# Output projection that starts on attention's half while the recurrence's rows are gated, and first routing weights split inside it

## The chip, the cores and the metric

The kernel runs on one core of one Trainium2 chip. The metric is the device time in microseconds; lower is better. The core has a matrix engine (TensorE; PE in the rows, with its weight loads as PEld), VectorE (DVE), ScalarE (ACT), GpSimd (POOL), and SyncE (SP), which here issues nearly all transfers. The engines run their own instruction streams and meet at semaphores.

## What is computed

One layer of a hybrid decoder on 512 tokens of width 2048, with 16 learned tokens in front: a projection into attention's and a recurrence's inputs, sliding window attention (8 heads of 128), a gated linear recurrence (8 heads of 128) whose outputs are normalised per head and multiplied with a gate, an output projection of both side by side (2048 x 2048), and then a feed-forward part that scores 16384 experts by product keys, picks 16 for each of 8 routing heads and mixes them. All in float32.

```
    _, o = lax.scan(_hgrn2_chunk_step, s0, xs)
    o = o.transpose(1, 0, 3, 2, 4).reshape(B, Lp, HGRN_HEADS, HGRN_DV)[:, pad:]
    o = rms_norm(o, norm_g.reshape(HGRN_HEADS, HGRN_DV)).reshape(B, L, HV)
    return (o * jax.nn.silu(hg.astype(jnp.float32))).astype(out_dtype)
...
        hn = rms_norm(h, ln_mix_g[l])
        proj = hn @ w_in[l]
        aq, ak, av, hq, hf, hi, hg = jnp.split(proj, split_at, axis=-1)
...
        att = sliding_window_sink_attention(aq, ak, av, attn_sinks[l])
        rec = hgrn2_mixer(hq, hf, hi, hg, lbs[l], hgrn_norm_g[l])
        h = h + jnp.concatenate([att, rec], axis=-1) @ w_out[l]
...
        h = h + peer_ffn(rms_norm(h, ln_ffn_g[l]), peer_w_q[l], peer_sub_keys[l], peer_u[l], peer_v[l])
```

## The kernel before

The kernel is a row of stages, each a block of its own: every engine runs its part of a block, and the next block begins when all are done. In order: norm_rows (first norm), project, attend, recur, mix_out (the output projection), norm_rows again (the norm in front of the feed-forward part), route, gate_table, experts. The first five are over at 1023 us of the profiled execution and the second norm at 1048.

**Numbers in two parts.** A float32 matrix product is done as three matmuls on numbers split into a high part (a cast to fp32r) and a low part (the rest): high by high, low by high, high by low (product, L341 to L345). So whatever TensorE multiplies is first split. Class Stream does it for weights: SyncE loads steps of 512 KB (2 chunks of 128 rows by 512 columns) into four raw slots, ScalarE casts the high part (L298; L304 for the first two steps of a stage), GpSimd subtracts for the low part (L312), each into one of two slots, and TensorE counts a step as used when its last matmul is done (used), which opens the slot to ScalarE again. A load into a raw slot waits until the low part that was read from it is done.

**recur.** Eight heads, one after the other, with all engines in turn. When a head's output is in PSUM (o_bank), ScalarE squares and sums it into stat (L1049) and copies it to mix (L1052), whose 2048 columns are attention's 1024 (chunks 0 to 7) and the recurrence's 1024 (chunks 8 to 15). After the last head: SyncE starts the first four loads of w_out, VectorE turns the sums into means, ScalarE takes the root (L1084, with a table load), VectorE makes the reciprocal root (inverse_root, L102 to L106) and then gates: 32 scalar_tensor_tensor instructions of 128 x 128, one for each head and block of 128 tokens (L1231).

**mix_out.** TensorE transposes mix, chunk by chunk: 4 transposes of 128 x 128 each (L1274) into one of 4 PSUM banks; ScalarE casts a bank to mixT_high (L1298), VectorE subtracts to mixT_low (L1323), and the bank is free for chunk c + 4. When all 16 are done (`pe.wait_ge(low, DC)`), the product runs: 4 pieces of 512 output columns, each 8 steps of 2 chunks, each step 2 x 4 x 3 = 24 matmuls of 512 columns. For each piece VectorE adds x (L1333), which SyncE loads into h when all chunks are transposed (L1258; h lies where mix was), and ScalarE squares the sum for the next norm's means (L1304). SyncE's queue is in order: x, then w_out's other steps, then the first four loads of w_q, routing's weights.

**Second norm.** VectorE scales the rows (L206, four instructions of 128 x 2048), TensorE transposes them (L230), ScalarE and VectorE write the two parts (L171, L212). ScalarE and GpSimd split the first two steps of w_q here, ahead of their other work of this block (L168, L181); GpSimd then makes plain_rows (L2139).

**route.** TensorE computes the queries (first matmul L343 on x_high, w_q_hi) and scores head by head, VectorE picks the best 16s.

## Time and profile before

| what | us |
|---|---|
| median of 3 runs | 3577.05 |
| lowest, highest run | 3573.82, 3586.83 |
| device time of the profiled execution | 3564.46 |
| span of the profiled execution | 3562.6 |
| TensorE, VectorE, ScalarE, GpSimd busy in the span | 3357.4, 2235.9, 1118.1, 1162.3 |

Two kinds of view are used below. A timeline lists instructions by start, merges equal ones that follow each other ("x3" with their common length), and gives in brackets how long the engine had been idle and what released it (PEq L942 is the block's meeting point behind recur). Windows give the busy time of each engine in a stretch, and PEclk, the TensorE clock that was granted: 1.00 is 2.4 GHz, 0.50 is 1.2 GHz, and what lies between is a stretch with both. The times in a row are microseconds from the span's start, single durations in tile views nanoseconds.

### The profile page before, as it was taken

Reading aid. Unit: us, or ns where it says so; the run is one execution under the profiler, and the core shown is the slowest. Engines: PE = TensorE matmul, PEld = TensorE weight load, DVE = VectorE, ACT = ScalarE, POOL = GpSimd, SP = SyncE. Lnnn points to the kernel's source line nnn. Section 1 sums busy time; section 2 is a strip of 40 time slices with the busy share of each in tenths; the row PEclk is TensorE's granted clock in tenths of the full one; section 3 lists DMA queues with packets and bytes.
Section 4 is the critical chain, followed back from the end, with each engine's and each line's share of the span. In section 5 each row is a group of like instructions: output and inputs, shape, how many; then the busy total and the mean of one; then the engine's idle time right before and its main releaser. Section 6 shows DMA issues by size and latency. Waiting matters only on the chain.

```text
span 3562.6 us, 51459 instructions
## 1 busy us (share of the span) xinstructions
PE 3357.4 (94%) x16926; PEld 2941.1 (83%) x16926; DVE 2235.9 (63%) x3877; ACT 1118.1 (31%) x1732; POOL 1162.3 (33%) x870
## 2 busy tenths in 40 slices
PE   7999999777989947899999999999999999999999
PEld 5778876666868746799998998998998998998998
DVE  2003412794027899667777777777777777777676
ACT  3122223443232249332233223232233222222222
POOL 2344431263435510322322322323323333333332
PEclk9999999899999979999999999999999999999999
DMA  4233320003322124887887888887888888888876
GB/s 140 74 86 95 96 80 20 1 1 118 95 105 83 59 83 188 298 265 262 275 263 260 275 261 264 269 267 259 273 265 263 271 265 264 269 266 263 269 263 233
DMA packets 276020, 686.84 MB, mean 193 GB/s; under 512 B 120544, under 2 KB 120800, under 8 KB 273504
## 3 DMA queue, kind: packets, MB, share of 16 engines
q1 hardware_dynamic: 202224, 417.51, 36.2%
q0 software_dynamic: 73728, 268.47, 22.5%
q8 instruction: 37, 0.61, 0.1%
q14 instruction: 31, 0.25, 0.0%
HBM read 655.48 MB, written 30.41 MB: 193 GB/s over the span
## 4 chain that ended last, share of the span: by engine, by line
PE 59%; ACT 2%; issue 1%; DMA 1%; ACTq 0%; DVE 0%; DVEq 0%; SPq 0%
PE exp_a L1864 10%; PE exp_a L1866 10%; PE exp_a L1865 10%; PE exp_o L1885 10%; PE exp_o L1887 10%; PE exp_o L1883 10%; ACT table_gaps L1682 1%; ACT table_stage L1698 1%; DMA gate_table<-table_stage 0%; PE table_b L1642 0%; ACTq L1682 0%; DMA exp_raw<-in_v 0%; ACTq L1698 0%; PE table_t L1633 0%; DVE table_hot L1668 0%
## 5 line engine op out<-in xcount | busy, mean ns | idle before, releaser
L1864 PE MATMUL exp_a<-x_high,exp_uh 128*128 128x384 f32 x2048 | 686.3, 335 | 10.0 <-DVE exp_ul L1948 10.0
L1866 PE MATMUL exp_a<-x_high,exp_ul 128*128 128x384 f32 x2048 | 685.8, 335 | 0.0
L1865 PE MATMUL exp_a<-x_low,exp_uh 128*128 128x384 f32 x2048 | 685.7, 335 | 0.0
L1887 PE MATMUL exp_o<-exp_vh,exp_al 128*128 128x512 f32 x1536 | 598.2, 389 | 0.0
L1885 PE MATMUL exp_o<-exp_vl,exp_ah 128*128 128x512 f32 x1536 | 598.1, 389 | 0.0
L1883 PE MATMUL exp_o<-exp_vh,exp_ah 128*128 128x512 f32 x1536 | 597.5, 389 | 0.0
L1843 POOL DMA_INDIRECT exp_rows<-in_v_rows,exp_now x256 | 326.8, 1277 | 710.1 <-DVE h L1969 658.6
L1843 POOL DMA_INDIRECT exp_rows<-in_u_rows,exp_now x256 | 299.9, 1171 | 732.1 <-DVE exp_rows L1962 687.1
L1913 ACT CAST exp_vh<-exp_raw 128x1024 fp32r<-128x1024 f32 x256 | 260.0, 1050 | 516.5 <-PE exp_o L1887 493.2
L1948 DVE TENSOR_TENSOR exp_vl<-exp_raw,exp_vh 128x1024 fp32r<-128x1024 f32 x256 | 304.6, 1220 | 164.7 <-ACT exp_vh L1913 164.7
L1864 PEld LDWEIGHTS exp_a<-x_high,exp_uh 128*128 128x128 f32 x2048 | 385.6, 188 | 11.7 <-DVE exp_ul L1948 7.3
L1865 PEld LDWEIGHTS exp_a<-x_low,exp_uh 128*128 128x128 f32 x2048 | 385.6, 188 | 1.2
L1866 PEld LDWEIGHTS exp_a<-x_high,exp_ul 128*128 128x128 f32 x2048 | 385.5, 188 | 0.0
L1924 ACT ACTIVATE exp_act<-exp_a 128x384 f32<-128x384 f32 x128 | 63.0, 492 | 962.3 <-PE exp_a L1866 962.3
L1887 PEld LDWEIGHTS exp_o<-exp_vh,exp_al 128*128 128x128 f32 x1536 | 288.3, 188 | 60.0
L1885 PEld LDWEIGHTS exp_o<-exp_vl,exp_ah 128*128 128x128 f32 x1536 | 288.3, 188 | 59.3
L1883 PEld LDWEIGHTS exp_o<-exp_vh,exp_ah 128*128 128x128 f32 x1536 | 288.3, 188 | 59.2
L1948 DVE TENSOR_TENSOR exp_ul<-exp_raw,exp_uh 128x1024 fp32r<-128x1024 f32 x256 | 309.8, 1221 | 41.5 <-ACT exp_uh L1913 31.5
L312 POOL TENSOR_TENSOR w_in_lo<-w_in_raw,w_in_hi 128x1024 fp32r<-128x1024 f32 x88 | 212.9, 2419 | 332.6 <-ACT w_in_hi L298 332.6
L1969 DVE SCALAR_TENSOR_TENSOR h<-exp_rows,exp_weights,h 128x1024 f32<-128x1024 f32 x256 | 316.5, 1277 | 0.0
L1962 DVE SCALAR_TENSOR_TENSOR exp_rows<-exp_rows,sparse_x 128x1024 f32<-128x1024 f32 x256 | 302.4, 1218 | 0.0
L1989 DVE TENSOR_TENSOR exp_act<-exp_act,exp_gates 128x384 f32<-128x384 f32 x128 | 71.9, 562 | 360.3 <-ACT exp_act L1924 360.3
...
## 6 DMA issues: line engine op xcount, KB each, us to landing
exp_raw<-in_u SPq DMA_DIRECT2D x256, 512.0 KB, 5.3
exp_raw<-in_v SPq DMA_DIRECT2D x256, 512.0 KB, 4.4
...
exp_gates<-gate_table SPq DMA_DIRECT2D x128, 192.0 KB, 5.3
...
```

The lines of the kernel that those rows point to most:

```text
L312: eng.tensor_tensor(self.lo[:, g % 2], self.raw[:, g % RAW], self.hi[:, g % 2].bitcast(F32), ALU.subtract).then_inc(self.low, 1)
L1843: pool.indirect_dma_start(rows[slot][:, :], None, sparse["u" if kind == "dot" else "v"], bass.IndirectOffsetOnAxis(ap=now[:, turn, place_n ...
L1864: pe.matmul(bank, uh[:, b, c, :], xh[:, 0:DENSE_TB, c, :], start=(c == 0), stop=False)
L1865: pe.matmul(bank, uh[:, b, c, :], xl[:, 0:DENSE_TB, c, :], start=False, stop=False)
L1866: last = pe.matmul(bank, ul[:, b, c, :], xh[:, 0:DENSE_TB, c, :], start=False, stop=(c == DC - 1))
L1883: pe.matmul(bank[:, :], ah[:, key, tokens], vh[:, dc % 2, key, :], start=(key == 0), stop=False)
L1885: pe.matmul(bank[:, :], ah[:, key, tokens], vl[:, dc % 2, key, :], start=False, stop=False)
L1887: last = pe.matmul(bank[:, :], al[:, key, tokens], vh[:, dc % 2, key, :], start=False, stop=(key == KEYS_OF_MACRO - 1))
L1913: act.copy(part(uh if split[0] == "u" else vh, *split, half), raw[:, c % RAW_SLOTS, :])\
L1948: dve.tensor_tensor(part(ul if kind == "u" else vl, kind, which, half), raw[:, slot, :], part(uh if kind == "u" else vh, kind, which, half ...
L1962: done = dve.scalar_tensor_tensor(rows[slot][:, :], rows[slot][:, :], 1.0, sparse["x"][:, half, :], ALU.mult, ALU.mult, accum_out=dots[:, ...
L1969: done = dve.scalar_tensor_tensor(sums, rows[slot][:, :], weights[:, pl(pick(m, kind, t), 1)], sums, ALU.mult, ALU.add)
```

## The change

Nothing that is computed changes. The tail of recur moves into mix_out, and mix_out no longer waits for all of it.

- recur ends with ScalarE's last copy to mix. Its first four loads of w_out are issued when recur begins (the raw slots move to the half of `turned` that recur doesn't read, the split parts take the other half).
- mix_out transposes attention's chunks 0 to 7 first, and its product begins on them. ScalarE takes the root behind the second cast; VectorE splits the eight chunks, then does inverse_root and the 32 gatings, now head by head, with a count after each head (gated), and then the low parts of chunks 8 to 15. TensorE transposes those behind steps 1, 2 and 3 (counted from 0) of the first piece (TURN_AFTER: 2, 3 and 3 chunks), each waiting for its head's gating. The first piece is written out of the loop.
- SyncE issues w_out's steps 4 to 7 ahead of x.
- The first two steps of w_q are split at the end of mix_out (ScalarE ahead of the last four squares, GpSimd behind its last step), not in the second norm.

TensorE, before, where recur ends and mix_out begins:

```order
L942 UNCONDITIONAL_BRANCH
L1267 UNCONDITIONAL_BRANCH
L1274 MATMUL out_t<-c_ident,mix 128x128 x64
L1278 UNCONDITIONAL_BRANCH
L1278 ISA
L1285 ISA
L343 MATMUL out_bank<-w_out_hi,mixT_high 128x512
```

and in the changed kernel the same place:

```order
L949 UNCONDITIONAL_BRANCH
L1261 UNCONDITIONAL_BRANCH
L1271 MATMUL out_t<-c_ident,mix 128x128 x32
L350 MATMUL out_bank<-w_out_hi,mixT_high 128x512
L351 MATMUL out_bank<-w_out_hi,mixT_low 128x512
L352 MATMUL out_bank<-w_out_lo,mixT_high 128x512
```

Half of the 64 transposes now stand ahead of the first product; the others follow it in groups of 8, 12 and 12.

VectorE, before, the same place (rec_stat is stat, L1231 the gating, mixT_low the low parts):

```order
L1222 TENSOR_SCALAR rec_stat<-rec_stat 128x32
L102 RECIPROCAL rec_stat<-rec_stat 128x32
L103 TENSOR_TENSOR rec_stat<-rec_stat 128x32
L104 TENSOR_TENSOR rec_stat<-rec_stat 128x32
L105 TENSOR_SCALAR rec_stat<-rec_stat 128x32
L106 TENSOR_TENSOR rec_stat<-rec_stat 128x32
L1231 SCALAR_TENSOR_TENSOR mix<-mix,rec_stat,nat 128x128 x32
L942 UNCONDITIONAL_BRANCH
L1318 UNCONDITIONAL_BRANCH
L1323 TENSOR_TENSOR mixT_low<-out_t,mixT_high 128x512 x16
```

and changed:

```order
L949 UNCONDITIONAL_BRANCH
L1336 UNCONDITIONAL_BRANCH
L1345 TENSOR_SCALAR rec_stat<-rec_stat 128x32
L1342 TENSOR_TENSOR mixT_low<-out_t,mixT_high 128x512 x8
L102 RECIPROCAL rec_stat<-rec_stat 128x32
L103 TENSOR_TENSOR rec_stat<-rec_stat 128x32
L104 TENSOR_TENSOR rec_stat<-rec_stat 128x32
L105 TENSOR_SCALAR rec_stat<-rec_stat 128x32
L106 TENSOR_TENSOR rec_stat<-rec_stat 128x32
L1356 SCALAR_TENSOR_TENSOR mix<-mix,rec_stat,nat 128x128 x32
L1342 TENSOR_TENSOR mixT_low<-out_t,mixT_high 128x512 x8
```

The root and the gating now stand behind the block's meeting point and between two halves of the low parts.

GpSimd, before, where mix_out ends and the second norm begins:

```order
L319 COMPARE_AND_BRANCH
L1243 UNCONDITIONAL_BRANCH
L177 UNCONDITIONAL_BRANCH
L312 TENSOR_TENSOR w_q_lo<-w_q_raw,w_q_hi 128x1024 x2
L2139 TENSOR_TENSOR plain_rows<-scaled_rows,ln_ffn_row 128x2048
```

and changed:

```order
L326 COMPARE_AND_BRANCH
L319 TENSOR_TENSOR w_q_lo<-w_q_raw,w_q_hi 128x1024 x2
L1234 UNCONDITIONAL_BRANCH
L178 UNCONDITIONAL_BRANCH
L2176 TENSOR_TENSOR plain_rows<-scaled_rows,ln_ffn_row 128x2048
```

The two splits of w_q have moved ahead of the block's meeting point.

The diff, cut where lines only follow from the rest:

```diff
--- before.py
+++ after.py
@@ -165,7 +165,8 @@
...
             act.wait_ge(meaned, 1)
             act.activation(stat[:, 2, 0:n], stat[:, 1, 0:n], ACT.Sqrt).then_inc(rooted, 1)
-            stream.split_first_high(act)
+            if split_here:
+                stream.split_first_high(act)
...
@@ -178,7 +179,8 @@
...
-            stream.split_first_low(pool)
+            if split_here:
+                stream.split_first_low(pool)
...
@@ -264,12 +266,13 @@
-    def __init__(self, nc, tag, place, kb, src, span=SPAN):
+    def __init__(self, nc, tag, place, kb, src, span=SPAN, parts_kb=None):
...
-        self.hi = place(f"{tag}_hi", [P, 2, span, cols], F32R, kb + 16)
-        self.lo = place(f"{tag}_lo", [P, 2, span, cols], F32R, kb + 24)
+        parts_kb = kb + 16 if parts_kb is None else parts_kb
+        self.hi = place(f"{tag}_hi", [P, 2, span, cols], F32R, parts_kb)
+        self.lo = place(f"{tag}_lo", [P, 2, span, cols], F32R, parts_kb + 8)
...
-    def load_rest(self, sp, pieces):
+    def load_first(self, sp):
         for g in range(RAW, self.steps):
             self.load(sp, 0, g)
+
+    def load_rest(self, sp, pieces, begun=False):
+        if not begun:
+            self.load_first(sp)
         with sp.Fori(1, pieces) as p:
             for g in range(self.steps):
                 self.load(sp, p, g)
...
@@ -1003,7 +1008,6 @@
         @block.sync
         def _(sp):
-            sp.wait_ge(squared, TB * RH)
             stream.load_start(sp)
...
@@ -1080,8 +1084,6 @@
             by_pairs(act, head)
             copy_out(RH - 1)
-            act.wait_ge(meaned, 1)
-            act.activation(stat[:, 2], stat[:, 1], ACT.Sqrt).then_inc(rooted, 1)
...
@@ -1216,28 +1218,17 @@
             gap_to_end(0)
             by_pairs(dve, head)
-            outs = mix[:, :, QH * HD:].rearrange("p t (j h d) -> p t j h d", j=2, d=HD)
-            gates = nat[:, HG_PIECE:HG_PIECE + 2, :, :].rearrange("p j t (h d) -> p j t h d", d=HD)
-            dve.wait_ge(squared, TB * RH)
-            dve.tensor_scalar(stat[:, 1], stat[:, 0], 1.0 / HD, EPS, ALU.mult, ALU.add)\
-                .then_inc(meaned, 1)
-            dve.wait_ge(rooted, 1)
-            tail = Count(dve, mix_ready)
-            inverse_root(dve, tail.link, stat[:, 3], stat[:, 1], stat[:, 2], stat[:, 0])
-            dve.wait_ge(out_copied, RH + 1)
-            for tb in range(TB):
-                for h in range(RH):
-                    head = outs[:, tb, h // 4, h % 4, :]
-                    dve.scalar_tensor_tensor(head, head, stat[:, 3, tb, h:h + 1],
-                                             gates[:, h // 4, tb, h % 4, :], ALU.mult, ALU.mult)
...
-def mix_out(nc, place, stream, mix, mixT, h, x, cst, sums, next_loads):
+AHEAD = DC // 2
+TURN_AFTER = {1: (8, 10), 2: (10, 13), 3: (13, 16)}
+
+
+def mix_out(nc, place, stream, mix, mixT, h, x, cst, sums, next_stream, nat, stat):
...
@@ -1254,49 +1246,72 @@
         @block.sync
         def _(sp):
+            stream.load_first(sp)
             sp.wait_ge(turned, DC)
             sp.dma_start(h[:, :, :], x.rearrange("(b p) d -> p b d", p=P)).then_inc(x_loaded, 16)
-            stream.load_rest(sp, OUT_PIECES)
-            next_loads(sp)
+            stream.load_rest(sp, OUT_PIECES, begun=True)
+            next_stream.load_start(sp)
         @block.gpsimd
         def _(pool):
             stream.split_first_low(pool)
             stream.split_low_rest(pool, OUT_PIECES)
+            next_stream.split_first_low(pool)
         @block.tensor
         def _(pe):
             stream.start_free(pe)
-            for c in range(DC):
+
+            def turn(c):
                 if c >= 4:
                     pe.wait_ge(low, c - 3)
+                if c >= AHEAD:
+                    pe.wait_ge(gated, c - AHEAD + 1)
                 for tb in range(TB):
                     last = pe.transpose(t_bank[c % 4][:, tb, :], mix[:, tb, c * P:(c + 1) * P],
                                         cst["ident"][:, :])
                 last.then_inc(turned, 1)
-            pe.wait_ge(low, DC)
-            with pe.Fori(0, OUT_PIECES) as p:
+
+            def step(p, g, first):
+                stream.await_step(pe, p, g)
+                for s in range(SPAN):
+                    c = g * SPAN + s
+                    if first:
+                        pe.wait_ge(low, c + 1)
+                    for tb in range(TB):
+                        if c == 0:
+                            pe.wait_ge(added, p * TB + (tb + 1))
+                        tokens = slice(tb * P, (tb + 1) * P)
+                        last = product(pe, banks[tb][:, :], (hi[:, c, tokens], lo[:, c, tokens]),
+                                       stream.parts(g, s), c == 0, c == DC - 1)
+                        if c == DC - 1 and tb < TB - 1:
+                            last.then_inc(unit_done, 1)
+                stream.release(last)
+
+            for c in range(AHEAD):
+                turn(c)
+            for g in range(STEPS):
+                step(0, g, True)
+                for c in range(*TURN_AFTER.get(g, (0, 0))):
+                    turn(c)
+            with pe.Fori(1, OUT_PIECES) as p:
                 for g in range(STEPS):
-                    stream.await_step(pe, p, g)
-                    for s in range(SPAN):
-                        c = g * SPAN + s
-                        for tb in range(TB):
-                            if c == 0:
-                                pe.wait_ge(added, p * TB + (tb + 1))
-                            tokens = slice(tb * P, (tb + 1) * P)
-                            last = product(pe, banks[tb][:, :], (hi[:, c, tokens], lo[:, c, tokens]),
-                                           stream.parts(g, s), c == 0, c == DC - 1)
-                            if c == DC - 1 and tb < TB - 1:
-                                last.then_inc(unit_done, 1)
-                    stream.release(last)
+                    step(p, g, False)
         @block.scalar
         def _(act):
             stream.split_first_high(act)
-            for c in range(DC):
+
+            def high_part(c):
                 act.wait_ge(turned, c + 1)
                 act.copy(hi[:, c, :], t_bank[c % 4][:, :, :].rearrange("p b t -> p (b t)"))\
                     .then_inc(high, 1)
+
+            for c in range(AHEAD):
+                high_part(c)
+                if c == 1:
+                    act.wait_ge(meaned, 1)
+                    act.activation(stat[:, 2], stat[:, 1], ACT.Sqrt).then_inc(rooted, 1)
             def square(p, tb):
                 act.wait_ge(added, p * TB + (TB + tb + 1))
@@ -1307,21 +1322,42 @@
             act.sem_inc(squared, 1)
             for g in range(2, STEPS):
                 stream.split_high(act, 0, g)
+                for c in range(*TURN_AFTER.get(g - 2, (0, 0))):
+                    high_part(c)
             with act.Fori(1, OUT_PIECES) as p:
                 for g in range(STEPS):
                     stream.split_high(act, p, g)
                     if 1 <= g <= TB:
                         square(p - 1, g - 1)
+            next_stream.split_first_high(act)
             for tb in range(TB):
                 square(OUT_PIECES - 1, tb)
         @block.vector
         def _(dve):
             dve.sem_inc(added, TB)
-            for c in range(DC):
+
+            def low_part(c):
                 dve.wait_ge(high, c + 1)
                 dve.tensor_tensor(lo[:, c, :], t_bank[c % 4][:, :, :].rearrange("p b t -> p (b t)"),
                                   hi[:, c, :].bitcast(F32), ALU.subtract).then_inc(low, 1)
+
+            dve.tensor_scalar(stat[:, 1], stat[:, 0], 1.0 / HD, EPS, ALU.mult, ALU.add)\
+                .then_inc(meaned, 1)
+            for c in range(AHEAD):
+                low_part(c)
+            dve.wait_ge(rooted, 1)
+            inverse_root(dve, Count(dve, chain).link, stat[:, 3], stat[:, 1], stat[:, 2], stat[:, 0])
+            outs = mix[:, :, QH * HD:].rearrange("p t (j h d) -> p t j h d", j=2, d=HD)
+            gates = nat[:, HG_PIECE:HG_PIECE + 2, :, :].rearrange("p j t (h d) -> p j t h d", d=HD)
+            for k in range(RH):
+                for tb in range(TB):
+                    head = outs[:, tb, k // 4, k % 4, :]
+                    last = dve.scalar_tensor_tensor(head, head, stat[:, 3, tb, k:k + 1],
+                                                    gates[:, k // 4, tb, k % 4, :], ALU.mult, ALU.mult)
+                last.then_inc(gated, 1)
+            for c in range(AHEAD, DC):
+                low_part(c)
             dve.wait_ge(x_loaded, 16)
             with dve.Fori(0, OUT_PIECES) as p:
                 for tb in range(TB):
@@ -2059,7 +2095,8 @@
     nat_meta = place("nat_meta", [M, META_PIECES, PC], F32, 154)
     turned = place("turned", [P, 2 * RH, L], F32, 160)
     mixT = [place("mixT_high", [P, DC, T], F32R, 66), place("mixT_low", [P, DC, T], F32R, 98)]
-    w_out = Stream(nc, "w_out", place, 160, a["w_out"])
+    w_out = Stream(nc, "w_out", place, 176.5, a["w_out"], parts_kb=160)
+    head_stat = place("rec_stat", [P, 4, TB, RH], F32, 133)
     keys = place("rec_keys", [P, RH, L], F32, 32)
     logs = place("rec_logs", [P, RH, L], F32, 48.5)
     x_rows = place("x_rows", [P, TB, D], F32, 98)
@@ -2151,11 +2188,12 @@
                       place, 138, w_in, load_rows, (early_in, 16 * len(early)), pool_first=narrow_mask)
     spent = project(nc, place, 176.5, w_in, hn, nat, nat_meta, meta_row, turned, cst, spent)
     attend(nc, place, 66, nat, nat_meta, turned, keys, logs, mix, cst, load_keep, keep_in, spent)
-    recur(nc, place, 32, 98, nat, nat_meta, turned, keys, logs, mix, cst, w_out)
-    mix_out(nc, place, w_out, mix, mixT, h, a["x"], cst, sums, w_q.load_start)
+    recur(nc, place, 32, 98, nat, nat_meta, turned, keys, logs, mix, cst, w_out, head_stat)
+    mix_out(nc, place, w_out, mix, mixT, h, a["x"], cst, sums, w_q,
+            nat, head_stat)
     norm_rows(nc, "ffnnorm", [h[:, tb, :] for tb in range(TB)], [scaled_rows[:, tb, :] for tb in range(TB)],
               None, cst["ln_ffn"], xT, lambda part, c: part[:, :, c, :], cst["ident"], place, 136, w_q,
-              load_keys, sums=sums, pool_last=plain)
+              load_keys, sums=sums, pool_last=plain, split_here=False)
     route(nc, place, 136, w_q, xT, picks, cst, plain_stored)
     def load_u(sp, key, half, slot):
```

## Rows read from the trace of the kernel before

**Rows 1.** Timeline, ScalarE, stage meeting; columns: start, length (us), operation, xcount, [idle].

```profile
823.55 0.59 ACT L1052 COPY mix<-rec_o 128x512 f32<-128x512 f32 x1
824.15 1.28 ACT L1084 ACT_TABLE_LOAD   x1
...
835.76 1.99 ACT L304 CAST w_out_hi<-w_out_raw 128x1024 fp32r<-128x1024 f32 x2 [10.09 <-PEq L942]
837.66 1.69 ACT L1298 CAST mixT_high<-out_t 128x512 fp32r<-128x512 f32 x3
```

**Rows 2.** Timeline, VectorE, the same stretch.

```profile
825.71 0.35 DVE L102 RECIPROCAL rec_stat<-rec_stat 128x32 f32<-128x32 f32 x1 [1.98 <-ACT rec_stat L1084]
...
826.99 8.49 DVE L1231 SCALAR_TENSOR_TENSOR mix<-mix,rec_stat,nat 128x128 f32<-128x128 f32 x32
838.27 2.66 DVE L1323 TENSOR_TENSOR mixT_low<-out_t,mixT_high 128x512 fp32r<-128x512 f32 x4 [2.79 <-ACT mixT_high L1298]
841.09 7.35 DVE L1323 TENSOR_TENSOR mixT_low<-out_t,mixT_high 128x512 fp32r<-128x512 f32 x12 [0.17 <-ACT mixT_high L1298]
```

**Rows 3.** Timeline, TensorE, the same stretch; last row its weight loads (PEld).

```profile
821.52 0.39 PE L1099 MATMUL rec_o<-rec_state,rec_q_in 128*128 128x128 f32 x2
835.93 10.83 PE L1274 MATMUL out_t<-c_ident,mix 128*128 128x128 f32 x64 [14.03 <-PEq L942]
848.78 0.49 PE L343 MATMUL out_bank<-w_out_hi,mixT_high 128*128 128x512 f32 x1 [2.02 <-DVE mixT_low L1323]
...
842.52 0.42 PEld L1274 LDWEIGHTS out_t<-c_ident,mix 128*128 128x128 f32 x4 [0.27 <-DVE mixT_low L1323]
```

**Rows 4.** Timeline, TensorE: end of projection, second norm, start of routing.

```profile
1022.76 0.39 PE L345 MATMUL out_bank<-w_out_lo,mixT_high 128*128 128x512 f32 x1
1030.75 1.54 PE L230 MATMUL ffnnorm_bank<-c_ident,scaled_rows 128*128 128x128 f32 x6 [7.60 <-DVE scaled_rows L206]
...
1048.93 0.66 PE L343 MATMUL route_q<-x_high,w_q_hi 128*128 128x512 f32 x1 [3.71 <-PEq L124]
```

**Rows 5.** Windows: stretch, length, busy PE PEld DVE ACT POOL, PEclk, DMA share, GB/s.

```profile
799.00:800.00 1.00, 0.41 (x3) 0.41 (x4) 1.00 (x2) 0.00 (x0) 0.26 (x1) 0.93 0.00 0
...
803.00:804.00 1.00, 1.00 (x9) 1.00 (x8) 0.66 (x2) 0.82 (x2) 0.52 (x1) 0.86 0.00 0
...
828.00:832.00 4.00, 0.00 (x0) 0.00 (x0) 4.00 (x17) 0.00 (x0) 0.00 (x0) 0.50 0.59 242
```

**Rows 6.** Timeline, VectorE: L206 in the second norm (two rows), the first norm.

```profile
1027.30 3.40 DVE L206 TENSOR_SCALAR scaled_rows<-h,ffnnorm_stat 128x2048 f32<-128x2048 f32 x1
...
1033.90 1.27 DVE L206 TENSOR_SCALAR scaled_rows<-h,ffnnorm_stat 128x2048 f32<-128x2048 f32 x1
...
19.47 4.88 DVE L206 TENSOR_SCALAR x_rows<-x_rows,mixnorm_stat 128x2048 f32<-128x2048 f32 x4
```

**Rows 7.** Timeline, GpSimd: last split of the projection, splits in second norm.

```profile
1013.44 2.39 POOL L312 TENSOR_TENSOR w_out_lo<-w_out_raw,w_out_hi 128x1024 fp32r<-128x1024 f32 x1 [3.05 <-ACT w_out_hi L298]
1027.27 5.63 POOL L312 TENSOR_TENSOR w_q_lo<-w_q_raw,w_q_hi 128x1024 fp32r<-128x1024 f32 x2 [11.44 <-ACT w_q_hi L304]
```

**Rows 8.** Timeline, ScalarE, second norm.

```profile
1037.11 9.36 ACT L171 ACTIVATE x_high<-ffnnorm_bank,c_ln_ffn 128x512 fp32r<-128x512 f32 x16 [8.97 <-PE ffnnorm_bank L230]
```

**Rows 9.** Timeline, inside the recurrence: VectorE's L1169 twice, and one of GpSimd.

```profile
811.41 0.83 DVE L1169 TENSOR_TENSOR rec_halves<-rec_decays,turned 128x256 f32<-128x256 f32 x1
...
817.02 0.42 DVE L1169 TENSOR_TENSOR rec_halves<-rec_decays,turned 128x256 f32<-128x256 f32 x1
...
811.17 0.79 POOL L1024 TENSOR_TENSOR rec_gaps<-rec_logs 128x256 f32<-128x256 f32 x1
```

**Rows 10.** Tile h, 840 to 900 us: duration ns min/median/max, first and last start.

```profile
L1333 DVE TENSOR_TENSOR h<-h,out_bank x4: 686/689/689, 890.7 to 892.7; 128x512 f32 x4
...
DMA to landing us min/median/max: 12.4/12.4/12.4
```

**Rows 11.** Tile w_out_raw, whole span, the same columns: its transfers' time to landing.

```profile
DMA to landing us min/median/max: 3.5/3.7/14.0
```

9 lines of the change are left out of this document (4 added, 5 removed).

## The prediction, as put on record before the changed kernel ran

> **What bounds the kernel now.** TensorE sets the end: it is busy for 3357.4 of the 3562.6 us, and its long idle stretches lie where stages meet. So I read the timeline of each engine where recur and mix_out meet, then where mix_out and the second norm meet. Every stage waits for the one before, so a microsecond saved there is saved at the end, unless a later stage has a limit of its own. At the first place the reader should follow one chain. TensorE's last output product of recur starts at 821.52 and then TensorE does nothing until 835.93 [rows 3]. Meanwhile ScalarE copies to mix until 824.14, loads a table and takes a root (to 825.7) [rows 1], VectorE makes the reciprocal root (825.71 to 826.99) and gates for 8.49 us, to 835.48 [rows 2]. Only then does mix_out begin: ScalarE at 835.76, so 0.28 later [rows 1], TensorE 0.45 later. Sixteen chunks are transposed and split, and the first product stands at 848.78 [rows 3]. From ScalarE's last copy to the first product 24.64 us pass, in which TensorE does nothing of the product, though half of its left operand (attention's) has long been ready. From there on TensorE has no gap: 768 matmuls from 848.78 to 1022.76 [rows 3, 4] are 0.2268 us apart, 5.44 for a step of 24.
>
> **Part 1, the start of mix_out.** I rebuild the stretch from the same durations. recur ends at 824.14 (last copy), so ScalarE starts at 824.42 and TensorE at 824.59. ScalarE's two weight casts put its first mixT_high 1.90 later, at 826.32; the next follows 0.55 later and ends at 827.46 [rows 1]. Now comes the root: table load and root took from 824.15 to 825.71, 1.56 [rows 1, 2], so the third cast starts at 829.02. A low part starts 0.61 after its high part, and VectorE makes one each 0.61 (twelve in 7.35 [rows 2], each about 0.68 long): the low part of chunk 2 starts at 829.63, that of chunk 3 ends at 830.92. The transposes of chunk 7 wait for that bank, and four transposes take 0.42 when nothing holds them [rows 3]: 831.34. The first product then needs mixT of chunks 0 and 1 only, and the weights' low part: GpSimd needs 2.39 for a step [rows 7], from about 825.5, so 827.9. The first product starts at **831.4**, which is 17.4 earlier.
>
> **Part 2, what is put in.** 8 x 4 transposes now lie inside the product on TensorE. At 0.42 a chunk that is **3.4** given back. Do they wait? The low part of chunk 7 ends at 833.4, the reciprocal root 1.28 later, the 32 gatings another 8.49 later, at 843.1, the first head at about 835.8. Steps 0 and 1 end at 831.4 + 10.9 = 842.3 at the earliest, so the transposes of chunks 8 and 9 find their heads gated. Chunk 12 is the first that needs a bank back from a low part made behind the gating (chunk 8's, about 844); TensorE comes to it after step 2, at 848.6 or later. Some 5 us cover both, and if they were gone each microsecond would count. ScalarE's casts of chunks 8 to 15 stand behind its weight casts, 1.0 each [rows 1] in a step of 5.44, so it stays far ahead. GpSimd has the same 2.39 in 5.44.
>
> Here is one thing that speaks against the change: the gating now shares its stretch with GpSimd's weight split. In the recurrence an equally large instruction of VectorE took 0.83 while GpSimd worked beside it and 0.42 when GpSimd was through [rows 9], so VectorE can double. All 32 gatings doubled would end at 851.6 and hold chunk 12 by some 4 us; but in those 8.5 us GpSimd splits one step of 2.39, so the sum takes 0, and at most 2.4 longer gating, which the 5 us cover. The Trainium skill (SBUF — State Buffer, section Who interferes with whom) has a rule for this: a VectorE instruction with two SBUF inputs contends with a GpSimd instruction that reads SBUF, and one waits for the other's whole instruction. By that rule one gating waits once for up to a whole split, which is the same 2.4; the rows agree in direction, and the sum is the same by either.
>
> **Part 3, the clock.** The sum so far assumes 2.4 GHz. Before, TensorE idle from 822 found its clock at 0.50 in 828 to 832 [rows 5]. There it cost little, since ScalarE and VectorE set the pace. In the new order TensorE is idle for 2.7 us and then has eight short bursts in 7 us, so I expect a fall as well, but now it meets the product. A low spell in the recurrence lasted from 799.9 to 803.3 (PEclk 0.93 in one window, 0.86 in the other) [rows 5], 3.4 us at half rate: **1.7** lost. The ends are 0 (it stays high, or the spell ends before the product) and 3.4 (two spells or a longer one).
>
> **Part 4, the second norm.** VectorE scales four row blocks. Beside GpSimd's two weight splits the first took 3.40; the third, without them, 1.27; in the first norm four took 4.88 together [rows 6]. GpSimd's two splits, in turn, took 5.63 where two would take 4.78 [rows 7]. With the splits gone to mix_out, the four take 4.88 as in the first norm and not 1036.4 - 1027.3 = 9.1 (the fourth follows the third by 1.2), a gain of 4.2. It can't all be had: TensorE, at its low clock here, took 1.54 for 6 transposes [rows 4], some 0.24 each. Now it would start at 1028.6, and the 18 that stand ahead of the first whole bank take 4.3; with 0.5 for the last one and the hand-over ScalarE starts at 1033.4 instead of 1037.11 [rows 8]: **3.7**. The rest of the norm goes on at VectorE's pace as before, and routing's first matmul (1048.93 [rows 4]) moves by as much. The splits in mix_out are free: ScalarE has cast w_out's last step at 1013.4, GpSimd is through with it at 1015.8 [rows 7], and 2 x 2.39 more end at 1020.6, before TensorE's last matmul. w_q's first steps are asked for right behind w_out's last load, and half of such loads land within 3.7 [rows 11], so they are there. If it were not free, ScalarE's 2 us would push the last squares.
>
> **Part 5, transfers.** w_out's first 2 MB now load beside the start of recur, where nothing else is loaded. x is asked for when chunk 15 is transposed: 831.4 + 1.7 + 4 x 5.44 + 3.4 = 858.3, and took 12.4 to land [rows 10], so 870.7. The first add of piece 0 was at 890.7 [rows 10], 41.9 behind the first product: now 878.4. 7.7 to spare. Behind x in the queue comes w_out's piece 1, whose longest landing was 14.0 [rows 11]: 872.6. Its split can begin when step 6 is used, at 874.6, and has 2.0 more before the product needs it: 4.0 to spare. So 0.
>
> **The sum.** -17.4 + 3.4 + 1.7 - 3.7 = **-16.0 us**. On the profiled execution 3564.46 becomes 3548.5 (span 3546.6). That execution is 12.6 below the median of the three runs, which scatter over 13 us; the difference is taken off the median: 3577.05 - 16.0 = **3561.0**.
>
> **Rivals.**
> - *The clock stays high.* For it: TensorE is now wholly idle for 2.7 us, not for 14. Then nothing is lost in part 3: -17.7, 3559.3; with a norm gain of the full 4.2, -18.2. Against it: the low spell of the recurrence began with TensorE busy for 0.41 of the microsecond before [rows 5], so less than a long idle stretch brings the clock down. 0.22.
> - *The norm gives less.* TensorE's transposes at half clock or the wait for them set the start of the norm, and only 1 to 2 us of 3.7 come; or the low spell in the product is twice as long. -13, 3564. 0.2.
> - *A later stage takes most of it back*, since something there (a transfer, GpSimd's gathers) runs to a time of its own. The profile shows routing led by TensorE and VectorE and the experts by TensorE without gaps, so this is unlikely: -5, 3572. 0.06.
> - *Slower: x and piece 1's weights land late.* They are asked for 11 us later in the program than the work that they follow, when the product is already half through its first piece. Landing 4.0 later than the longest seen stalls TensorE, and the kernel is slower than before once the delay is over 20 us, with a landing of 34 us against 14.0. A delay of 25 us would give 3582. 0.03.
> - *It doesn't do what it says*: the transposes of chunks 8 and 9 wait for the whole gating, because a wait is in the wrong place. The order shows them behind step 1 and one count for each head, and even the whole gating is over at 843.1, 1 us after step 1: -15. That is inside the forecast.
>
> **How the numbers follow.** The forecast has 0.49. The bounds of its own terms are -18.2 and -13, the scatter of a median adds some 4 us on both sides, so 3555 to 3569 holds the forecast and the first two rivals in most cases; to hold 8 in 10 I give 3554 to 3570. A measurement of this kernel can tell about 0.5% from no change, that is 17.9 us. The forecast is just below that: faster by more has the larger part of the first rival and a quarter of the forecast by scatter, 0.3; slower by more 0.03, the last but one rival; within it 0.67.
>
> **What would show it.** TensorE's first product 7.3 us (5 to 9) behind ScalarE's last copy to mix, and no wait at the transposes of chunks 8 to 15. VectorE's four scalings in the second norm 1.28 each; if they take longer, part 4 is wrong. PEclk below 1.00 for 3 to 4 us within the first two steps; if it is 1.00 throughout, part 3 is. TensorE without a gap at the end of the first piece, or part 5 is. And the distance from routing's first matmul to the end unchanged within 2 us.

## The result, and the profile after

| | kernel before | changed kernel |
|---|---|---|
| median of 9 runs | 3579.62 | 3550.87 |
| lowest, highest | 3573.82, 3587.51 | 3540.65, 3565.65 |
| span of the profiled execution | 3562.6 | 3549.1 |
| recur's last copy to mix ends | 824.14 | 827.77 |
| first product of the output projection | 848.78 | 835.22 |
| first product of routing | 1048.93 | 1036.75 |

The ratio is 0.9936, 95% interval 0.9918 to 0.9954: faster by 0.64%, or by 16.5 to 29 us of 3579.62. The two traces differ by 13.5 us. From the start of recur's last copy to routing's first product, the stretch that the change rewrites, it is 225.4 before and 209.6 after: **15.8 us** less, where the prediction had 16.0.

The timeline of the changed kernel where recur and mix_out meet (columns as in the rows of before), ScalarE first [rows 1]:

```profile
827.19 0.58 ACT L1056 COPY mix<-rec_o 128x512 f32<-128x512 f32 x1
828.06 2.01 ACT L311 CAST w_out_hi<-w_out_raw 128x1024 fp32r<-128x1024 f32 x2 [0.28 <-PEq L949]
829.97 1.06 ACT L1307 CAST mixT_high<-out_t 128x512 fp32r<-128x512 f32 x2
831.04 1.28 ACT L1314 ACT_TABLE_LOAD   x1
```

The casts follow the last copy after 0.28, and the root, which stood ahead of mix_out, now stands behind the second cast. VectorE's gating and GpSimd's splits of w_out [rows 2, 7]:

```profile
838.11 8.49 DVE L1356 SCALAR_TENSOR_TENSOR mix<-mix,rec_stat,nat 128x128 f32<-128x128 f32 x32
849.13 1.29 DVE L1342 TENSOR_TENSOR mixT_low<-out_t,mixT_high 128x512 fp32r<-128x512 f32 x2 [2.54 <-ACT mixT_high L1307]
...
829.18 4.67 POOL L319 TENSOR_TENSOR w_out_lo<-w_out_raw,w_out_hi 128x1024 fp32r<-128x1024 f32 x2 [12.83 <-ACT w_out_hi L311]
843.26 7.94 POOL L319 TENSOR_TENSOR w_out_lo<-w_out_raw,w_out_hi 128x1024 fp32r<-128x1024 f32 x2 [9.41 <-ACT w_out_hi L305]
```

The 32 gatings take 8.49 as before. GpSimd's first two splits take 4.67, about 2.4 each. But its third starts at 843.26 and the two of that row end at 851.20; the fourth takes 2.39, so the third took some 5.6 and ended at 848.8, 2.2 behind the last gating (846.60). TensorE [rows 3]:

```profile
833.81 1.76 PE L1271 MATMUL out_t<-c_ident,mix 128*128 128x128 f32 x8 [1.24 <-DVE mixT_low L1342]
835.22 0.78 PE L350 MATMUL out_bank<-w_out_hi,mixT_high 128*128 128x512 f32 x1
...
847.31 1.03 PE L1271 MATMUL out_t<-c_ident,mix 128*128 128x128 f32 x8
848.89 0.50 PE L350 MATMUL out_bank<-w_out_hi,mixT_high 128*128 128x512 f32 x1 [0.54 <-POOL w_out_lo L319]
```

The first product is 7.45 behind the end of the last copy (24.64 before). At 847.31 are the transposes of chunks 8 and 9, which wait for nothing; at 848.89 the third step waits 0.54 for GpSimd. The low clock begins in the last transposes and ends in the first step of the product; windows of 1 us [rows 5]:

```profile
834.00:835.00 1.00, 1.00 (x7) 0.91 (x7) 1.00 (x3) 0.74 (x3) 0.00 (x0) 0.54 0.60 172
835.00:836.00 1.00, 1.00 (x5) 0.90 (x4) 1.00 (x2) 0.73 (x2) 0.00 (x0) 0.50 0.83 193
836.00:837.00 1.00, 1.00 (x3) 0.79 (x3) 0.92 (x3) 0.20 (x1) 0.00 (x0) 0.50 0.68 279
837.00:838.00 1.00, 1.00 (x5) 0.73 (x4) 0.86 (x5) 0.00 (x0) 0.00 (x0) 0.75 0.04 16
```

In the second norm, VectorE's four scalings [rows 6], GpSimd's splits of w_q, now in mix_out [rows 7], ScalarE's first high part [rows 8], and routing's first product [rows 4]:

```profile
1019.24 4.88 DVE L208 TENSOR_SCALAR scaled_rows<-h,ffnnorm_stat 128x2048 f32<-128x2048 f32 x4
...
1007.74 4.74 POOL L319 TENSOR_TENSOR w_q_lo<-w_q_raw,w_q_hi 128x1024 fp32r<-128x1024 f32 x2
...
1024.94 9.35 ACT L172 ACTIVATE x_high<-ffnnorm_bank,c_ln_ffn 128x512 fp32r<-128x512 f32 x16 [6.74 <-PE ffnnorm_bank L232]
...
1036.75 0.77 PE L350 MATMUL route_q<-x_high,w_q_hi 128*128 128x512 f32 x1 [3.71 <-PEq L124]
```

The scalings take 4.88 together (9.1 before). From the last add's start to routing's first product pass 21.6 us instead of 25.6. From there to the end of the span it is 2512.4 against 2513.7.

### The profile page after: what moved, and what is told of

Its sections match the earlier page's. It is cut to its first block, busy times and chain, and to the rows that moved or that the text cites. A ratio compares the mean times of both kernels' runs of the same rounds, so it can differ in the third digit from the quotient of the medians.

```text
span 3549.1 us, 51460 instructions
## 1 busy us (share of the span) xinstructions
PE 3359.0 (95%) x16926; PEld 2944.6 (83%) x16926; DVE 2226.8 (63%) x3877; ACT 1116.9 (31%) x1732; POOL 1165.7 (33%) x870
## 4 chain that ended last, share of the span: by engine, by line
PE 59%; ACT 2%; issue 1%; DMA 1%; ACTq 0%; DVE 0%; DVEq 0%; SPq 0%
PE exp_a L1900 10%; PE exp_a L1902 10%; PE exp_a L1901 10%; PE exp_o L1921 10%; PE exp_o L1923 10%; PE exp_o L1919 10%; ACT table_gaps L1718 1%; ACT table_stage L1734 1%; DMA gate_table<-table_stage 0%; PE table_b L1678 0%; ACTq L1718 0%; DMA exp_raw<-in_v 0%; ACTq L1734 0%; DVE table_hot L1704 0%; PE table_t L1669 0%
## 5 line engine op out<-in xcount | busy, mean ns | idle before, releaser
L1900 PEld LDWEIGHTS exp_a<-x_high,exp_uh 128*128 128x128 f32 x2048 | 385.8, 188 | 12.3 <-DVE exp_ul L1984 7.3
```

The source lines that it names most:

```text
L1900: pe.matmul(bank, uh[:, b, c, :], xh[:, 0:DENSE_TB, c, :], start=(c == 0), stop=False)
```

## The experiments

Seven kernels were timed against the kernel before, the changed one again among them; two more, and the kernel before again, were profiled only. "The stretch" is always that from the start of recur's last copy to routing's first product.

### The change again, and each half alone

Three kernels: the changed one; the changed start of mix_out with w_q's splits left in the second norm; and the kernel before with only w_q's splits moved. The start alone, on the changed kernel:

```diff
             stream.split_low_rest(pool, OUT_PIECES)
-            next_stream.split_first_low(pool)
...
-            next_stream.split_first_high(act)
             for tb in range(TB):
...
-              load_keys, sums=sums, pool_last=plain, split_here=False)
+              load_keys, sums=sums, pool_last=plain)
```

The norm alone puts the same three lines into the kernel before, and leaves its start of mix_out as it was:

```diff
             stream.split_low_rest(pool, OUT_PIECES)
+            next_stream.split_first_low(pool)
...
+            next_stream.split_first_high(act)
             for tb in range(TB):
...
-              load_keys, sums=sums, pool_last=plain)
+              load_keys, sums=sums, pool_last=plain, split_here=False)
```

Expected of the change again:

> The changed kernel once more, beside the others. The two traces explain 15.8 us of gain up to routing's first matmul (11.7 in the output projection, 4.1 in the second norm), while the first comparison of medians gave 23 +- 6. Theory A, the gain is those 15.8 us and the rest is scatter of the clock in the stages before: ratio 0.9955 to 0.9960, 16 us. Theory B, there is a further gain of some 7 us that these stretches do not hold: ratio 0.9935 again, and a stretch behind routing's first matmul that is shorter than before in this trace too.

Expected of the start alone:

> The change without its second part: the first two steps of routing's weights are split in the second norm, as before. Theory A: the output projection keeps its 11.7 us, the second norm takes from the last adds to routing's first matmul 27.7 us again, not 23.6; 12 us faster than before, ratio 0.9966. If the two parts depend on each other (the norm gained because the clock or the timing differs), the norm is shorter than 27.7 here too.

Expected of the norm alone:

> The kernel before with only the second part: the first two steps of routing's weights are split at the end of the output projection. Theory A: the four scalings of rows take 4.9 us together instead of 9.1, the norm is 4.1 us shorter, 3570-ish against 3574-ish, ratio 0.9989. Rival: GpSimd's two splits beside the end of the product delay the last adds, and the output projection is 1 to 2 us longer, total under 3 us.

Measured:

| kernel | the stretch | less than 225.4 | ratio to before, interval |
|---|---|---|---|
| change again | 209.6 | 15.8 | 0.9943, 0.9924 to 0.9962 |
| start only | 213.5 | 11.9 | 0.9950, 0.9932 to 0.9968 |
| norm only | 222.5 | 2.9 | 0.9990, 0.9978 to 1.0002 |

The first ratio, with its interval, does not tell the two theories of the change again apart. The start alone gained the 12 us that were expected in the stretch; its ratio came out further from 1 than the expected 0.9966, which its interval just holds. The norm alone is in time not clear of no change, as expected, and shows in the trace only.

The halves add up to 14.8 of 15.8. The missing microsecond is a clock spell that fell elsewhere. With the norm alone the four scalings are at 1.28 each (the tile scaled_rows: ns min/median/max, first and last start), so the norm gave its full gain; but windows at the beginning of its output projection show this:

```profile
L208 DVE TENSOR_SCALAR scaled_rows<-h,ffnnorm_stat x4: 1281/1282/1286, 1044.8 to 1048.4; 128x2048 f32<-128x2048 f32 x4
```

```profile
866.00:867.00 1.00, 1.00 (x4) 0.77 (x3) 0.00 (x0) 0.00 (x0) 0.00 (x0) 0.53 1.05 434
...
868.00:869.00 1.00, 1.00 (x4) 0.81 (x3) 0.00 (x0) 0.00 (x0) 0.00 (x0) 0.50 0.93 393
869.00:870.00 1.00, 1.00 (x4) 0.81 (x4) 0.00 (x0) 0.00 (x0) 0.00 (x0) 0.76 1.08 459
```

TensorE was at half clock from 866 to about 869.8, inside the product, where the kernel before ran its first steps at full clock. From first product to last add are 176.1 us instead of 174.5, so 1.6 are lost there (the rival had expected such a loss at the end of the product; it is at the start). From last add to routing are 21.5 instead of 25.6, so the norm's own gain is 4.1. The order of work at the product's start is the same in both. So a low spell of 3 to 4 us there is nothing that only the new order brings; where it falls differs.

### Does the early load of w_out matter?

The changed kernel asks for w_out's first four parts at the start of recur, not at its end. This puts the wait back, and keeps all else:

```diff
         def _(sp):
+            sp.wait_ge(squared, TB * RH)
             stream.load_start(sp)
```

> The changed kernel with the first four loads of the output projection's weights issued as before, when the last head's squares are done. In the trace before the change the loads took 3.8 to 6.3 us from that moment, so the first arrives about 4 us after it, 3.4 us behind the start of the block. Theory A: ScalarE's first weight cast waits some 3 us, and all behind it, the first product is 3 us later than in the changed kernel (10.5 us behind the last copy to mix instead of 7.45), ratio about 0.9965. Rival: the early load costs something in the recurrence (its first transfers beside the stage's start), which this gives back: the recurrence 1 us shorter, total the same as the changed kernel.

Measured: 3556.21, ratio 0.9951 (0.9936 to 0.9967); recur takes 147.6 as in the changed kernel, so neither load time changes it. ScalarE in the timeline:

```profile
824.10 0.59 ACT L1057 COPY mix<-rec_o 128x512 f32<-128x512 f32 x1
828.16 1.05 ACT L311 CAST w_out_hi<-w_out_raw 128x1024 fp32r<-128x1024 f32 x1 [3.48 <-DMA w_out_raw<-in_w_out]
829.46 1.05 ACT L311 CAST w_out_hi<-w_out_raw 128x1024 fp32r<-128x1024 f32 x1 [0.25 <-DMA w_out_raw<-in_w_out]
```

The first cast now waits for the transfer until 828.16, 3.2 later behind the copy than in the changed kernel, and the first product stands 3.8 later (11.2 behind the copy's end, where 10.5 was expected). The stretch is 213.1, 3.5 longer. So by the traces 3.5 of the gain come from the early load alone, which the ratio, with its interval, can't tell from the changed kernel; my part 5 had named the transfers only as a risk, and part 1 used the early load without pricing it.

### The kernel before again, and the gating twice

The unexpected 5.6 us of GpSimd's third split called for a theory. Mine: while VectorE's gatings run back to back, GpSimd doesn't get in between them, and its split is done only after the last. The rival: it is slowed for another reason, by the transfers or by its own queue. The kernel with each gating computed twice, the extra one into a buffer that nobody reads, doubles the train:

```diff
                     head = outs[:, tb, k // 4, k % 4, :]
+                    dve.scalar_tensor_tensor(twice[:, k, tb, :], head, stat[:, 3, tb, k:k + 1],
+                                             gates[:, k // 4, tb, k % 4, :], ALU.mult, ALU.mult)
```

> The changed kernel with each of the 32 gatings written once more, to a scratch tile ahead of the real one, so the train of gatings is 17.0 us long and not 8.5. In the changed kernel GpSimd's third weight split took some 5.6 us instead of 2.4 and ended 2.3 us after the last gating. Lock theory (GpSimd gets no turn until the train of two-input instructions is over): here it starts 15.5 us behind the last copy to mix and ends 29.7 us behind it, 14 us long, TensorE waits 9 us for it in front of its third step, and the output projection is 8.5 us longer. Sharing theory (the two slow each other by a factor): the split takes 5.6 us again, ends at 21.1, and TensorE waits some 2 us, for the low part of chunk 8, later.

GpSimd's third and fourth splits in its timeline, and the product's matmuls from 825 to 875 with what they waited for:

```profile
853.44 17.58 POOL L319 TENSOR_TENSOR w_out_lo<-w_out_raw,w_out_hi 128x1024 fp32r<-128x1024 f32 x2 [7.91 <-ACT w_out_hi L305]
```

```profile
L350 PE MATMUL out_bank<-w_out_hi,mixT_high 128*128 128x512 f32 x23 | 9.9, 432 | 10.2 <-POOL w_out_lo L319 10.2
```

64 gatings from 849.60, 0.263 apart, end at 866.5. GpSimd's two splits took 17.58. With 2.39 for the second, the first took 15.2 and ended 2.1 behind the train. TensorE stood 10.2 us for it. Beside it VectorE kept its pace: 0.34 a gating, 0.26 from one to the next, as without GpSimd. So the lock-out by this train is shown, and while the train runs it is GpSimd alone that pays.

It doesn't follow for every train. In the kernel before, VectorE's low parts of mixT [rows 2] also ran back to back from 838.27, beside GpSimd's first two splits, which took no longer than elsewhere:

```profile
836.88 4.70 POOL L312 TENSOR_TENSOR w_out_lo<-w_out_raw,w_out_hi 128x1024 fp32r<-128x1024 f32 x2 [24.17 <-ACT w_out_hi L304]
```

Of a low part's two inputs one, out_t, lies in PSUM; both inputs of a gating lie in SBUF. That this makes the difference fits the two traces, but it wasn't varied by itself.

The kernel before, once more, for the scatter of a trace:

> The kernel before, for a second trace of it. Theory A (what the two parts do is 15.8 us, the rest of the measured difference is the granted clock in the stages around): from the last copy to mix to routing's first matmul 225 us again, as in the first trace (225.4) and against 209.6 and 209.7 in the two traces of the changed kernel; attend, recur and route differ from the first trace by a few us each, and where they are longer PEclk is lower there. Theory B (the change shortens route too): route 201 us or longer in this trace and 199 in all of the changed kernel's.

Its stretch was 225.3, within 0.1 of the first. Outside of it, it was not so. Windows over attention, where nothing is changed, in the first trace of before, in that of the changed kernel and in this one (where attention takes longer, and the window with it):

```profile
590.00:676.00 86.00, 73.98 (x408) 57.60 (x406) 57.40 (x131) 44.73 (x120) 0.00 (x0) 0.89 0.00 1
```

```profile
590.00:676.00 86.00, 73.99 (x398) 58.42 (x398) 57.27 (x129) 44.58 (x120) 0.00 (x0) 0.85 0.00 1
```

```profile
590.00:689.00 99.00, 88.40 (x399) 69.60 (x398) 57.19 (x129) 45.25 (x120) 0.00 (x0) 0.71 0.00 1
```

The mean clock was 0.89, 0.85 and 0.71, and attention took 79.0, 81.8 and 93.5 us. The part is the same code in all three. What sets the clock in it is not settled by these runs. Of the 18.4 us between the spans of the two traces of before, 14.5 lie in attention and 4.8 in routing.

### Two edits that should bring the product forward

The root behind the eighth cast and not the second, so that the table load is not in the way of the first low parts; and, in another kernel, transposes that nobody reads ahead of the product, so that TensorE is never idle for long and keeps its clock:

```diff
-                if c == 1:
+                if c == AHEAD - 1:
                     act.wait_ge(meaned, 1)
```

```diff
             outputs(RH - 1, 1)
+            for _ in range(20):
+                pe.transpose(g_bank[0][:, 0, :], ident[:, :], ident[:, :])
...
                 turn(c)
+                if c in (3, 5):
+                    for _ in range(9):
+                        pe.transpose(banks[3][:, 0:P], cst["ident"][:, :], cst["ident"][:, :])
```

> The changed kernel with ScalarE's root behind the eighth cast of mixT_high and not behind the second. By the trace, the table load and the root (1.5 us) then no longer hold casts 2 to 7: first product 5.8 us behind the last copy to mix and not 7.45, and VectorE, which needs the root only after its eighth low part, starts the gating no later than before. 1.6 us faster than the changed kernel, ratio to the kernel before about 0.994. Rival: the gating starts later (root 1 us behind the eighth cast) and GpSimd's third split with it, which gives half of it back at the third step.

> The changed kernel with transposes that nobody reads put into TensorE's idle time: 20 behind the recurrence's last output, 9 behind the transposes of chunk 3 and 9 behind those of chunk 5. Clock theory: the granted clock fell to 1.2 GHz from 834.1 to 837.5 because of that idle time and cost 1.6 us in the first step; kept busy, it stays at 1.00 there, the first step takes 5.45 us and not 7.0, 1.6 us faster than the changed kernel. Rival: the fall comes anyway (from the pause at the stages' meeting, which can't be filled wholly) or the added transposes delay the real ones; then same or 1 us slower.

Root later: the first product is 5.8 behind the copy's end (7.45), 1.6 gained, and the clock's low spell is over before it, which gains another 1.1. VectorE's gatings, GpSimd, and the product with its waits:

```profile
838.81 8.49 DVE L1356 SCALAR_TENSOR_TENSOR mix<-mix,rec_stat,nat 128x128 f32<-128x128 f32 x32
...
842.04 9.79 POOL L319 TENSOR_TENSOR w_out_lo<-w_out_raw,w_out_hi 128x1024 fp32r<-128x1024 f32 x2 [6.62 <-ACT w_out_hi L305]
```

```profile
L350 PE MATMUL out_bank<-w_out_hi,mixT_high 128*128 128x512 f32 x47 | 19.3, 411 | 2.4 <-POOL w_out_lo L319 2.4
```

The third split ends at 849.4, again 2.1 behind the train (847.30), and TensorE, which is there earlier, waits 2.4 for it. Behind that wait the clock falls to 0.50 from 850 to 853.5. The stretch is 210.3, 0.7 longer than in the changed kernel: the gain is given back, and more, ratio 0.9937 (0.9916 to 0.9959).

Kept busy, the same rows and the clock in three windows:

```profile
838.52 8.50 DVE L1361 SCALAR_TENSOR_TENSOR mix<-mix,rec_stat,nat 128x128 f32<-128x128 f32 x32
...
842.37 9.20 POOL L319 TENSOR_TENSOR w_out_lo<-w_out_raw,w_out_hi 128x1024 fp32r<-128x1024 f32 x2 [7.91 <-ACT w_out_hi L305]
```

```profile
L350 PE MATMUL out_bank<-w_out_hi,mixT_high 128*128 128x512 f32 x48 | 19.7, 411 | 1.8 <-POOL w_out_lo L319 1.8
```

```profile
834.00:849.00 15.00, 13.19 (x66) 10.68 (x64) 13.60 (x45) 5.33 (x9) 7.09 (x2) 1.00 0.19 62
849.00:850.00 1.00, 0.71 (x3) 0.58 (x4) 0.54 (x1) 0.00 (x0) 1.00 (x2) 0.90 0.00 0
850.00:851.00 1.00, 1.00 (x4) 0.81 (x3) 0.00 (x0) 0.00 (x0) 1.00 (x1) 0.50 0.75 135
```

PEclk is 1.00 through the first two steps, so the fall is gone as meant. But the third step waits 1.8 for GpSimd, and behind that stall the clock falls after all. The stretch is 211.0, 1.4 longer than in the changed kernel, the ratio 0.9932 (0.9907 to 0.9957). Both edits work where they are made and gain nothing. The next limit is the third step's low part, which is tied to the end of the gatings, and a clock spell of some 1.6 us comes on top of the wait. The spell isn't bound to a wait of this size: in the start-only kernel TensorE waited 1.8 at the same place and kept its full clock behind it.

### A pause in the gatings

If that is so, VectorE should let GpSimd in:

```diff
             for k in range(RH):
                 for tb in range(TB):
+                    if k == 4 and tb == 0:
+                        dve.wait_ge(stream.low, 3)
                     head = outs[:, tb, k // 4, k % 4, :]
```

> The changed kernel, with one wait more: VectorE stops after 16 of its 32 gatings until GpSimd has made the low part of w_out's third step. Theory (GpSimd is locked out by the train of gatings and not slowed by it): its third split starts at about 843.3 as before and is done some 2.4 to 2.9 us behind its start (5.6 in the changed kernel), TensorE no longer waits for w_out_lo before the third step (0.54 in the changed kernel), the gatings end some 2.5 to 3 us later than 846.6, at about 849.5, and nobody waits for that; the stretch from recur's last copy to routing's first product is 209.1 (209.6 in the changed kernel). Rival (the split is slow for another reason, such as the writes of VectorE's results or its queue): the split still takes over 4 us while VectorE stands still.

VectorE's two halves of the gating, GpSimd's third and fourth splits, the product's start and the transposes of chunks 8 and 9 on TensorE, and the clock ahead of the product:

```profile
847.76 4.30 DVE L1358 SCALAR_TENSOR_TENSOR mix<-mix,rec_stat,nat 128x128 f32<-128x128 f32 x16
854.34 4.30 DVE L1358 SCALAR_TENSOR_TENSOR mix<-mix,rec_stat,nat 128x128 f32<-128x128 f32 x16 [2.28 <-POOL w_out_lo L319]
...
851.61 2.69 POOL L319 TENSOR_TENSOR w_out_lo<-w_out_raw,w_out_hi 128x1024 fp32r<-128x1024 f32 x1 [7.92 <-ACT w_out_hi L305]
857.05 3.85 POOL L319 TENSOR_TENSOR w_out_lo<-w_out_raw,w_out_hi 128x1024 fp32r<-128x1024 f32 x1 [2.74 <-ACT w_out_hi L305]
...
844.65 0.47 PE L350 MATMUL out_bank<-w_out_hi,mixT_high 128*128 128x512 f32 x1
...
855.66 1.03 PE L1271 MATMUL out_t<-c_ident,mix 128*128 128x128 f32 x8
```

```profile
838.00:839.00 1.00, 0.91 (x5) 0.94 (x6) 0.18 (x1) 1.00 (x2) 0.00 (x0) 0.50 0.00 0
...
841.00:842.00 1.00, 1.00 (x10) 1.00 (x9) 0.68 (x2) 1.00 (x1) 1.00 (x2) 0.85 0.00 0
842.00:845.00 3.00, 1.81 (x15) 1.35 (x13) 2.11 (x4) 2.97 (x8) 1.69 (x1) 1.00 0.79 191
```

The third split takes 2.69, the fourth, which starts beside the second half, 3.85; both end 2.2 behind a half's last gating (852.06 and 858.64). TensorE waits for neither. The stretch is 207.3, where 209.1 was expected. Of the 2.3 gained 0.8 is the wait: from the transposes of chunks 8 and 9 to those of the next three pass 6.34 us instead of 7.16. The rest is not this edit's but luck: the low spell of the clock was over at 841.7, three microseconds ahead of the product. That leaves the first product 7.05 behind the copy's end instead of 7.45, and 11.0 us instead of 12.1 from there to the transposes of chunks 8 and 9.

All three together:

> The changed kernel with the root behind the eighth cast, transposes into an unused bank that keep TensorE busy ahead of the product, and the pause in the middle of the gatings. Each of the first two alone brought the first steps forward by 1.5 and 1.6 us and lost it at the third step to GpSimd's late split. Theory: with the pause the third step finds its low part, so the gains add up: 209.6 - 1.5 - 1.6 - 0.5 = 206.0 from recur's last copy to routing's first product, 3.6 us less than in the changed kernel, no wait of TensorE for w_out_lo in the first piece, and PEclk at 1.00 until 855. The median then is 3547 to 3553 against 3551 to 3554 for the changed kernel, ratio to the kernel before 0.992 to 0.993; the trace decides, not the ratio, whose interval is as wide as the gain. Rival (something else is late next: the transposes of chunks 8 and 9 wait for the later gating, or chunk 12's bank for its low part): the same stretch stays at 208 or more, with a wait of TensorE for a gated head or for mixT_low.

GpSimd's third split, the product's waits and the clock from the first product on:

```profile
835.42 3.39 POOL L319 TENSOR_TENSOR w_out_lo<-w_out_raw,w_out_hi 128x1024 fp32r<-128x1024 f32 x1 [7.22 <-ACT w_out_hi L305]
```

```profile
L350 PE MATMUL out_bank<-w_out_hi,mixT_high 128*128 128x512 f32 x56 | 22.2, 396 | 0.0
```

```profile
828.00:870.00 42.00, 42.00 (x206) 35.24 (x205) 16.52 (x48) 12.77 (x18) 17.73 (x7) 1.00 0.50 183
```

Full clock for 42 us, no wait, the first product 6.8 behind the copy's end, and the stretch 206.7: 2.9 less than in the changed kernel, of 3.6 expected. The product starts 1.1 later than with the root later alone (5.8), so most of that gain isn't there; the added transposes, which TensorE does first, are the likely reason, not tested. Beside the pause alone (207.3) only 0.6 is left for the other two edits, but that trace had its clock spell in a harmless place. The median is 3547.81, ratio 0.9910 (0.9887 to 0.9932), the lowest ratio measured. That it beats the changed kernel is shown by the stretch, in one trace of it against two; the intervals of the ratios overlap.

## Why the prediction was right, and where it wasn't

**Part 1** (first product 7.3 behind the copy): 7.45. The chain of casts, low parts and bank hand-overs was added up from durations of before, and its order is the one in the trace. The 0.15 is two things that nearly cancel: the same start took 7.05 in four kernels whose last transposes ran at full clock or nearly (start only, gating twice, kept busy, pause), so the sum was 0.25 too long, and in the changed kernel the clock was already low in the last transposes (1.76 for the eight), which cost 0.4.

**Part 2** (8 chunks' transposes, 3.4): they cost 3.6 and waited for nothing. 3.6 is what the product takes longer than before in the pause kernel (178.1 against 174.5), which has neither the wait nor the low clock in it. The sentence that failed is the one on GpSimd: "has the same 2.39 in 5.44". I had asked only what GpSimd does to VectorE, by [rows 9], where a VectorE instruction doubled, and allowed the gating 2.4 us. It was the other way: the gating took 8.49 unslowed, and GpSimd's split 5.6. The Trainium skill (SBUF — State Buffer, Who interferes with whom) says that one of the two waits for the other's whole instruction. The trace agrees that one waits, and not on how long: beside the gatings it was always GpSimd, and it waited for a whole train of instructions, 13 of them in the changed kernel and some 50 with the gating twice. The price in the changed kernel is a wait of 0.54 by the profile, 0.8 from step to step, small only because TensorE came late enough: each microsecond that the product is brought forward meets this wait, as the two edits showed.

**Part 3** (clock, 1.7): a spell of 3.4 us at half clock, 834.1 to 837.5, cost 1.5: 0.4 ahead of the first product and 1.1 in it. The size was taken from a spell in recur and fits. But the cause wasn't the new order alone: the norm-only kernel had the same loss in the old order. And where the spell falls was luck. From the first product to the transposes of chunks 8 and 9 the two traces of the changed kernel took 12.1 and 12.0, the late load, with a longer spell, 13.1, and the six other kernels with this start 11.0, since their first spell lay ahead of the product or wasn't there. So a term of this kind was anything from 0 to 2.1 here.

**Part 4** (norm, 3.7): the stretch from last add to routing's product is 4.0 shorter, and ScalarE's first high part starts 5.7 behind the first scaling instead of 9.8, so 4.1. The bound by TensorE's transposes at low clock was 0.4 too cautious. The splits in mix_out took 4.74 and lay beside the product, as said.

**Part 5** (transfers, 0): right. TensorE has no wait at the first piece's end.

**The sum**: from the start of the last copy to the first product -17.2 (with 0.4 of clock in it), from there to the last add +5.5 (3.6 of transposes, 1.1 of clock and 0.8 of the wait), from there to routing -4.0. Together -15.8 with the roundings, against -16.0. So close a sum is in part luck: the wait for GpSimd, 0.8, which the sum put at nothing, was nearly made up for by a start, a clock spell and a norm that were each 0.2 to 0.3 better than their terms.

**The rivals**: the clock that stays high and the norm that gives less didn't come in the changed kernel; no later stage took anything back; nothing landed late. From routing's first product to the end it is 1.3 less than in the first trace of before, within the 2 us that the prediction allowed, and 4.6 less than in the second. The forecast's own case is what the trace shows up to routing.

**The level.** The forecast for the median was 3561.0, from 3554 to 3570; the median of nine runs is 3550.87, 10 lower and 3 under the range, though the stretch came out within 0.2. The median of before, with six more runs, rose from 3577.05 to 3579.62; as ratios the forecast is 0.9955 and the range's lower end 0.9936, which is what was measured. By the bound of 0.5% it is faster, which had 0.30, though the interval (0.46 to 0.82%) has the bound in it; the stretch alone would be 0.44%, on the other side. Two things lie in this. I set the level off a median of three runs that lay 13 us apart, and with the scatter allowed only 4 us on each side. And all kernels with the changed start gained more in time than in their stretch, while the norm alone hardly did (the gain by ratio is taken off 3577; its interval is some 6 us wide on each side, up to 9, so most rows by themselves are near its edge):

| kernel | less in the stretch | less by ratio |
|---|---|---|
| norm only | 2.9 | 4 |
| start only | 11.9 | 18 |
| late load | 12.3 | 18 |
| changed kernel, two batches | 15.8 | 20, 23 |
| root later | 15.1 | 23 |
| kept busy | 14.4 | 24 |
| all three | 18.7 | 32 |

A part of this sits in routing: TensorE's matmuls of routing with their waits, before and after, and a window of 25 us in each:

```profile
L343 PE MATMUL route_q<-x_high,w_q_hi 128*128 128x512 f32 x256 | 102.9, 402 | 12.8 <-POOL w_q_lo L312 9.1 <-PEq L124 3.7
```

```profile
L350 PE MATMUL route_q<-x_high,w_q_hi 128*128 128x512 f32 x256 | 102.8, 402 | 10.6 <-POOL w_q_lo L319 6.9 <-PEq L124 3.7
```

```profile
1148.90:1173.90 25.00, 21.45 (x91) 17.48 (x90) 23.31 (x106) 4.21 (x5) 12.63 (x6) 0.86 0.21 63
```

```profile
1136.80:1161.80 25.00, 23.71 (x113) 19.58 (x112) 21.69 (x114) 6.15 (x9) 14.34 (x6) 1.00 0.27 84
```

Before, TensorE waited 9.1 for w_q's low parts and the clock fell to 0.86 in this window; after, 6.9 and 1.00, though 50 us earlier it is the other way (1.00 before, 0.93 after). Routing's query products took 201.4, 206.2 and 207.7 in the three traces with the old start, and 198.1 to 199.2 in all nine with the new one. GpSimd's splits stand there behind products that wait for VectorE, so which split comes late depends on how the two meet; why the changed start should move that was not tried and stays open. So does the rest of the surplus. It must lie ahead of the last copy, since behind the query products all twelve traces take 2311 to 2315 us; there the copy starts anywhere from 821.1 to 839.8. The runs' mean clock is higher (0.978 against 0.974), but by an estimate from the windows 0.0015 of that is the change itself: where recur and mix_out meet TensorE's clock was low for some 14 us before, most of them idle, and is for 3.4 now.
